# Forgetting-branch gate projection moved between the units of the stick-breaking attention

## The reference

```python
def mixer(h, ...):
    proj = h @ w_in
    (q_r,k_r,v_r,g_r, q_s,k_s,v_s,g_s, q_f,k_f,v_f,g_f, f_logit) = split(proj)
    o_r = retention(rotary(q_r), rotary(k_r), v_r, state)      # 6 heads of 64
    o_s = stick_breaking(q_s, k_s, v_s)                        # 5 heads of 64
    logf = log_sigmoid(f_logit + b_f)
    o_f = forgetting_attention(rms(q_f), rms(k_f), v_f, cumsum(logf))
    o = concat([o_r*silu(g_r), o_s*silu(g_s), o_f*silu(g_f)])
    return o @ w_out
# stick breaking:  A[t,s] = sigmoid(z_ts) * prod_{s<j<t} (1 - sigmoid(z_tj)), s < t
```

## Time and profile before

| | us |
|---|---|
| median of three runs | 3687.98 |
| profiled execution, its time | 3678.38 |
| its span, first to last instruction | 3676.8 |
| TensorE busy | 3204.2 (87%) |
| VectorE busy | 1365.4 (37%) |
| ScalarE busy | 950.5 (26%) |
| GpSimd busy | 597.8 (16%) |

### The profile page before, as it was taken

The page is one execution under the profiler, slowest core; times in us unless marked ns, Lnnn a source line. Parts: engine busy times, 40 slices in busy tenths (PEclk is TensorE's granted clock), DMA queues, the critical chain, the costliest instruction groups (busy, mean ns, idle before and its releaser), DMA issues. The chain is left out here.

```text
span 3676.8 us, 67694 instructions
## 1 busy us (share of the span) xinstructions
PE 3204.2 (87%) x25256; PEld 1989.8 (54%) x25256; DVE 1365.4 (37%) x3002; ACT 950.5 (26%) x1746; POOL 597.8 (16%) x1090
## 2 busy tenths in 40 slices
PE   6999987888998688799989998978889987887998
PEld 4556654555666455444455666545556654554443
DVE  3235086443224444312142350954433244442211
ACT  2012144332224333211020122433322242331110
POOL 0000000444010044400000000004440101452000
PEclk9999988999999799899989999989999997998999
DMA  5011103887120388710120011048861205995102
GB/s 175 18 36 33 50 10 105 265 287 244 38 83 1 117 278 290 249 66 16 46 96 28 28 45 44 1 129 288 284 217 33 72 1 173 295 299 186 57 29 72
DMA packets 268657, 439.67 MB, mean 120 GB/s; under 512 B 48818, under 2 KB 216403, under 8 KB 268339
## 3 DMA queue, kind: packets, MB, share of 16 engines
q1 hardware_dynamic: 205810, 239.96, 20.4%
q0 software_dynamic: 55744, 189.25, 15.6%
q10 hardware_dynamic: 6912, 7.87, 0.6%
HBM read 410.28 MB, written 26.65 MB: 119 GB/s over the span
## 5 line engine op out<-in xcount | busy, mean ns | idle before, releaser
L806 PE MATMUL ps<-W,xT 128*128 128x320 f32 (+7 forms) x5120 | 1482.9, 465 | 11.5 <-DVEq L449 11.5
L806 PEld LDWEIGHTS ps<-W,xT 128*128 128x128 f32 (+1 forms) x5120 | 856.7, 184 | 585.6 <-issue 291.5
L688 POOL DMA_DIRECT2D branch<-in_cache_sb_v_dram x480 | 258.8, 539 | 637.5 <-issue 597.3
L688 POOL DMA_DIRECT2D branch<-in_cache_fox_v_dram x480 | 258.9, 539 | 621.2 <-issue 579.6
L1468 ACT ACTIVATE branch<-ps 128x512 f32<-128x512 f32 x288 | 165.6, 595 | 386.6 <-PE ps L1051 378.2
L1051 PE MATMUL ps<-C,W 128*128 128x128 f32 x1280 | 199.4, 301 | 73.1 <-DMA W<-in_cache_fox_k_dram 26.6
L1051 PE MATMUL ps<-C,branch 128*128 128x128 f32 x1280 | 194.9, 295 | 65.7 <-DMA branch<-in_cache_sb_k_dram 18.0
L1136 PE MATMUL ps<-branch 128*8 128x64 f32 x9920 | 182.2, 234 | 55.9 <-DMA branch<-in_cache_fox_v_dram 27.6
L1073 PE MATMUL ps<-branch,work 128*32 128x512 f32 x896 | 229.9, 631 | 0.8 <-issue 0.2
L1051 PEld LDWEIGHTS ps<-C,W 128*128 128x128 f32 x1280 | 151.0, 151 | 141.0 <-issue 67.4
L1051 PEld LDWEIGHTS ps<-C,branch 128*128 128x128 f32 x1280 | 147.8, 149 | 146.3 <-issue 96.1
(11 more groups left out here) (246 smaller groups left out, 3389.1 us busy)
## 6 DMA issues: line engine op xcount, KB each, us to landing
branch<-in_cache_sb_v_dram POOLq DMA_DIRECT2D x480, 160.0 KB, 4.3
branch<-in_cache_fox_v_dram POOLq DMA_DIRECT2D x480, 160.0 KB, 4.1
W<-in_cache_sb_k_dram SPq DMA_DIRECT2D x248, 160.0 KB, 3.4
W<-in_cache_fox_k_dram SPq DMA_DIRECT2D x248, 160.0 KB
branch<-in_cache_sb_k_dram SPq DMA_DIRECT2D x240, 160.0 KB, 4.2
branch<-in_cache_fox_k_dram SPq DMA_DIRECT2D x240, 160.0 KB, 4.3
W<-in_w_in_dram SPq DMA_DIRECT2D x14, 1280.0 KB, 6.3
W<-in_w_in_dram SPq DMA_DIRECT2D x9, 1536.0 KB, 7.1
```

The source lines that it names most:

```text
L688: pool.dma_start(ringV[:, g % 2, p * DA:(p + 1) * DA], cache[L, bass.ds(pg, 1)].rearrange("a s h d -> s (a h d)"))\
L806: ins = pe.matmul(out, src[:, k, t * P:t * P + R], W[i % 2][:, k, a:z], start=(k == 0), stop=(k == kc - 1), **place)
```

## The change

The nine `fg` tiles are projected within ATT_S, in pieces, in bank 7. Outputs of both attentions are now weighed in bank 6 alone and transposed into bank 7. The pieces and their places (i, h), each behind `turn` of that unit:

- tile 0: two k-steps each at (0,0), (0,1), (0,2), (0,3)
- tile k = 1 to 7: three at (k-1,4), three at (k,0), two at (k,1)
- tile 8 (sample rows): all eight at (7,4)

```diff
+ATT_FILL = {}                      # (i, h) -> (tile, first k-step, end)
+    _at = [(0, 0), (0, 1), (0, 2), (0, 3)] if _k == 0 else [(_k - 1, 4), (_k, 0), (_k, 1)]
+    _cut = [0, 2, 4, 6, KC] if _k == 0 else [0, 3, 6, KC] if _k < SAMPLE else [0, KC]
# banks
-    return 3 + 4 * (n % 2) if seg in IN_RET else n % 3
+    return 3 + 4 * (n % 2) if seg in IN_RET else 7 if seg == "fg" else n % 3
# weights: fq, fv -> W[0], fk -> W[1]; fq loaded once fg is projected
+W_OF = {seg: (0 if seg in ("fq", "fv") else 1 if seg == "fk" else i % 2) ...}
                 load_k(L, kind, 0, 0)
+                if kind == "sb":
+                    load_weights(L, "fq")
                 sp.wait_ge(phase_sem, 4 * ((ATT_S if kind == "sb" else ATT_F) + 1))
# TensorE, attention: weigh
-                    if c == 0 and i >= 2:
-                        pe.wait_ge(att_done[kind], i - 1)
+                    if c == 0 and i >= 1:
+                        pe.wait_ge(att_copied[kind], i)
# TensorE, back: bank 7, and
+                    if i >= 1:
+                        pe.wait_ge(att_done[kind], i)
+                    if kind == "sb":
+                        pe.wait_ge(emptied_dve, evac_count("fg", i + 1))
# TensorE, unit loop
-                    if h == 2 and i >= 1:
+                    if h == 3 and i >= 1:
                         back(t + 1)
                     turn(u)
+                    if kind == "sb" and (i, h) in ATT_FILL:
+                        k, first, end = ATT_FILL[i, h]
+                        if first == 0:
+                            if i >= 1:
+                                pe.wait_ge(att_done[kind], i)
+                            segment_start("fg", k, L)     # waits for tile k-1 emptied
+                        segment_steps("fg", k, first, end)
# ScalarE, unit loop, behind to_sbuf(u)
-                    if h == 1 and i >= 1:
+                    if h == 0 and i >= 1:
                         copy_out(t + 1)
+                    if kind == "sb" and h == 2 and i >= 1:
+                        gate_tile("fg", i)
+                    if kind == "sb" and (i, h) == (0, 4):
+                        gate_tile("fg", 0)
# VectorE, unit loop, behind stick(u)
+                    if kind == "sb" and h == 2 and i >= 1:
+                        gate_tile("fg", i)
+                    if kind == "sb" and (i, h) == (0, 4):
+                        gate_tile("fg", 0)
                     if h == 3 and i >= 1:
                         finish(t + 1)
# both, behind the units
+                if kind == "sb":
+                    gate_tile("fg", SAMPLE)
```

More of the change, by code:

```diff
@@ L62 @@
 TURNED = {"rq": TILES, "rk": TILES, "sq": NT, "sk": NT, "fq": NT, "fk": NT}
+W_OF = {seg: (0 if seg in ("fq", "fv") else 1 if seg == "fk" else i % 2) for i, seg in enumerate(ALL_SEGS)}
 GATE_AT = {"rg": 0, "sg": DR, "fg": DR + DA}
@@ L299, in step_program @@
         squares = cut(work, 2200, HA, HD)
-        logit = cut(work, 2600, TILES, HA)
+        logit = sb("logit", [P, TILES, HA])[:]
         ltmp = cut(work, 2650, TILES, HA)
@@ L578, in _ @@
                 sp.wait_ge(phase_sem, 4 * (DEC_S + 1))
-                load_weights(L, "fq")
+                load_weights(L, "fk")
                 load_decoded(L, "sb")
-                for seg in ALL_SEGS[10:13]:
+                for seg in ALL_SEGS[11:13]:
                     load_weights(L, seg)
@@ L781, in segment_tile, with segment_start @@
             def segment_tile(seg, t, L):
+                segment_start(seg, t, L)
+                segment_steps(seg, t, 0, PLE // P if seg[:2] == "pe" else KC)
+            def segment_start(seg, t, L):
                 i = ALL_SEGS.index(seg)
                 n = i * TILES + t
-                R, N = rows(t), SEG_W.get(seg, 512)
                 if t == 0 and seg == "rq":
@@ L795, in segment_tile @@
                     pe.wait_ge(norm_out, (TILES if seg == "pg0" else 0) + t + 1)
-                back = 2 if seg in IN_RET else 3
+                back = 2 if seg in IN_RET else 1 if seg == "fg" else 3
                 if n >= back:
@@ L800, in segment_tile, with segment_steps @@
                     pe.wait_ge(emptied_dve if s3 in DVE_EVACUATES else emptied_act, evac_count(s3, t3))
+            def segment_steps(seg, t, first, end):
+                R = rows(t)
                 src = pT if seg[:2] == "pe" else xT
                 kc = PLE // P if seg[:2] == "pe" else KC
-                for k in range(kc):
+                for k in range(first, end):
                     for out, a, z in pieces(seg, t):
                         place = dict(tile_position=(0, ROWS if a else 0), skip_group_check=True) if t == SAMPLE else {}
-                        ins = pe.matmul(out, src[:, k, t * P:t * P + R], W[i % 2][:, k, a:z],
+                        ins = pe.matmul(out, src[:, k, t * P:t * P + R], W[W_OF[seg]][:, k, a:z],
                                         start=(k == 0), stop=(k == kc - 1), **place)
-                ins.then_inc(proj_ready, 1)
+                if end == kc:
+                    ins.then_inc(proj_ready, 1)
             def turn_tile(seg, t):
@@ L1210, in _ @@
                 phase_over(pe, PROJ_S)
-                attention(ATT_S)
+                attention(ATT_S, L)
                 decode(DEC_S, L)
@@ L1214, in _ @@
                 phase_over(pe, PROJ_F)
-                attention(ATT_F)
+                attention(ATT_F, L)
                 decode(DEC_F, L)
@@ L1698, in project @@
                             link(dve.tensor_tensor(out, out, gated[0:R, t % 2, :], ALU.add))
[L1699 to L1704, removed]
+                        if seg == "fq" and t == 2:
+                            dve.wait_ge(logf_act, 2)
+                            dve.scalar_tensor_tensor(logf, logit, 0.0, ltmp, ALU.min, ALU.subtract)\
+                                .then_inc(logf_ready, 1)
+                    if seg == "fq":
                         dve.wait_ge(cum_ready, 1)
@@ L1847, in attention @@
                     link(dve.memset(prod[:, SEQ:SEQ + 1], 1.0))
+                    link(dve.memset(logit, 0.0))
                 def stick(u):
```

54 lines of the change are left out of this document (32 added, 22 removed).

## The result

The changed kernel takes 3754.94 us (median of four runs, 3740.71 to 3773.4) where the kernel before, run beside it, takes 3681.19 (3662.14 to 3694.21): a ratio of 1.0199, 95% interval 1.0168 to 1.023. It is slower, as forecast, but by about 74 us where 22 were forecast; 3755 lies above the range of 3670 to 3736.

The account below looks back on a forecast made before the run. The prediction took ATT_S as a chain over VectorE with TensorE close behind. Its terms, 43.4 + 3 + 8.8 + 1.5 - 45.6, made +11 us a layer, +22 in all: 3705 us, range 3670 to 3736.

Parts of the forecast that it names:

- The gate wait: In ATT_S, VectorE's gate of `fg` waits some 2.3 us for ScalarE's sigmoid, seven times.
- the layout: ATT_S instruction times laid out on paper, period by period: 115.6 us from `turn` (1,2) to (7,2), stage +43.4 us.
- Clock in ATT_S: Half clock behind TensorE's gaps in front of `turn` in ATT_S: +3 us a layer (0 to +6).
- the +59 that I gave as a bound: ATT_S growth if no filler found a gap and seven gate waits of 3.1 us came on top.
- the front: ATT_S up to `turn` (1,2): half clock, tile 0's gate and a wait for the emptied bank, +7.3 us.
- the end: End of ATT_S: sample tile, two sigmoid pieces and two products before the last `back`, +3.4 us.
- ATT_F: ATT_F: `back` at head 3 delays VectorE's finish and a chain behind it, +8.8 us (0, or +12 with clock losses).
- 45.6 in the sum: PROJ_F: us removed a layer, from the nine tiles, the `logf` wait, the sums and `fq`'s first tiles.
- the 7.9 for `logf` and the clock behind it: PROJ_F: 4.0 us wait for `logf`, 1.5 on the sums and 2.4 on `fq`'s first tiles removed.
- DEC_S: DEC_S: `fq`'s load holds SyncE's page loads, +2 us (0 to +4.7), less 0.5 for full clock: +1.5.
- Rival 3: Clock and DMA at their upper ends, ATT_S at 46: +23 us a layer, 3725 to 3735 us; chance 0.16.
- rival 1: Engines' slack takes the filler: ATT_S +25 us, -10 a layer, 3664 to 3680 us in all; chance 0.13.

Follow-up runs that it names:

- e1: Changed kernel with the `fg` gate, `back` and `finish` one unit later in ATT_S, all filler kept: 3704.22 us, ratio 1.0059 to the kernel before.
- e3: Changed kernel with 63 dummy transposes in all behind `back` in ATT_S, in TensorE's gaps: 3719.47 us, ratio 1.0118 to the kernel before.
- e10: Changed kernel, filler behind heads 2 to 4, gates behind head 0's `stick`, sigmoid and `back` reordered, ATT_F's `back` at head 2, `out0` load late: 3630.63 us.
- e2: Changed kernel with `back` at head 2 again in ATT_F alone: 3717.69 us, ratio 1.0103 to the kernel before.
- e6: Kernel before with only the `logf` chain moved beside `fq`'s tiles and the sums behind them, `fg` staying in PROJ_F: 3665.97 us, ratio 0.996.
- e5: Changed kernel with the load of `out0` held until PROJ_F's end: 3748.41 us, ratio 1.0173 to the kernel before.
- e9: e8 with each filler piece making only its first k-step, 46 of 72 k-steps a layer left out: 3638.2 us, ratio 0.9902 to the kernel before.
- e4: Changed kernel with each filler piece making only its first k-step, 46 of 72 left out a layer, waits kept: 3719.08 us, ratio 1.0108.
- e8: Changed kernel with the edits of e1, e2 and e5 together: 3668.48 us, ratio 0.9966 to the kernel before.

## Why the prediction was right and wrong

**The direction and its reason were right.** ATT_S is a chain over VectorE with TensorE close behind; the gate waits for a sigmoid that ScalarE's order puts late; and each engine waits in the other's heavy part. The gate wait has the size given (14.0 us in seven, 2.0 each, where I said about 2.3), the first `turn` stands at 7.16 against 7.1, and TensorE's gaps in front of it are 3.35, 2.88 and 2.42 us where the layout has 3.4, 3.0 and 2.5. e1's edit, which takes these waits away, gave back more than any other single one.

**The step that failed is "Clock in ATT_S", +3 (0 to +6).** The mechanism was the right one and its size was not. The layout's +43.4 leaves 20.5 us of ATT_S's +63.9 in layer 1 and 15.3 of +58.7 in layer 2; layer 1 even lies above the +59 that I gave as a bound. The distances from `turn` (k,2) to `turn` (k+1,2) in layer 1, read from the timelines, say where it was lost:

| us, for k = | 1 | 2 | 3 | 4 | 5 | 6 | sum |
|---|---|---|---|---|---|---|---|
| before | 19.6 | 17.1 | 14.8 | 12.4 | 10.0 | 9.3 | 83.2 |
| layout | 25.85 | 23.05 | 20.45 | 18.05 | 15.45 | 12.7 | 115.6 |
| after | 29.3 | 26.0 | 24.3 | 20.1 | 18.0 | 15.3 | 133.0 |
| e3, gaps filled | 26.1 | 23.6 | 21.0 | 18.4 | 18.2 | 15.4 | 122.6 |
| e10 | 22.3 | 19.9 | 17.5 | 15.2 | 13.1 | 11.2 | 99.2 |

In e3 the clock is at its full level through the first four periods, and there each distance comes within about 0.5 us of the layout. So the written order was laid out rightly and takes 87.4 us in these four. The kernel after takes 99.7, and filling the gaps gives back 10.7 of the 12.3 between them. In the last two periods both kernels have half level again and both are 5 us above the layout; that these 5 us are the clock's too is likely and was not tested. The term of +3 stands for 10.4 us shown in layer 1 and 7.2 in layer 2, and perhaps 16 in layer 1. Of the other pieces of the +43.4, the front has +8.9 / +3.4 for +7.3 and the end +5.3 / +5.1 for +3.4.

Half clock grew by 40.0 / 23.9 us. I charged the clock for the first 3 us behind the gap, as wide as the window in the earlier trace rows happened to be, and for little more than the first tiles. The traces show stretches of 6.8 to 10.2 us at the half level around each such gap, and they came for shorter gaps too: the same instruction in the later periods of the kernel after,

```profile
552.06 1.54 PE L986 MATMUL ps<-C,branch 128*128 128x128 f32 x6 [2.88 <-DVE branch L1912]
577.40 1.33 PE L986 MATMUL ps<-C,branch 128*128 128x128 f32 x5 [2.42 <-DVE branch L1912]
601.00 1.11 PE L986 MATMUL ps<-C,branch 128*128 128x128 f32 x4 [1.94 <-DVE branch L1912]
620.45 0.90 PE L986 MATMUL ps<-C,branch 128*128 128x128 f32 x3 [1.48 <-DVE branch L1912]
```

has half level from 551.4 to 558.2, 575.3 to 585.6, 599.2 to 606.0 and 619.7 to 626.5. The window 575 to 585 reads:

```profile
575.00:585.00 10.00, 7.60 (x34) 5.22 (x35) 8.36 (x11) 1.94 (x3) 0.00 (x0) 0.52 0.01 2
```

Ten us at half clock put TensorE some us behind in a period with no slack to catch up. The rule weighed in the prediction (the Trainium skill, "TensorE: Matmul & The Clock Gate", Why this matters for your kernels) names a longer gap than any of these four; by it none would have cost a clock. The measured rows decide, as I had chosen, and even so I charged too little.

**ATT_F: mechanism right, size too small.** TensorE's waits for the exponential and the copy behind it grew as said, by about one us each; the kernel after has 2.4 where the earlier trace rows have 1.37:

```profile
PE ps L1001 <- ACT work L1465: 14.9, 11, 2.4
PE ps L1001 <- ACT branch L1465: 8.8, 5, 2.4
```

Before, the two groups had 11.9 and 6.1 us, so the waits grew by 5.7. The rest of +17.1 / +12.8 goes with the clock: half level 67.3 / 46.9 us instead of 33.1 / 30.7; no run separates the two here. I had "+12 if clock losses follow" as the upper end, and it was too low. e2 takes nearly all of it away with one line.

**PROJ_F: TensorE's part right, an edit not costed.** Without the wait at its end the stage shrank by 44.9 us in both layers, for 45.6 in the sum, and L878 (the cumulative sums) has no wait. The sum came out though e6 gives back only 5.9 / 4.5 us of the 7.9 for `logf` and the clock behind it: in the whole change, 44.9 less the 37.6 of the tiles leaves 7.3. But I gave the order of the weight loads a sentence for `fk` and none for `out0`, whose 2048 KB moved from the middle of the stage to its last us, in front of a store that the barrier waits for: that wait grew by 3.9 / 3.7 us, and e5 gives back 3.4 / 3.1. The rule I cited for DEC_S (the Trainium skill, "DMA: Bandwidth & Descriptors", Issuing engines are not separate DMA queues) is what bears on this place: a load issued by SyncE held a store issued by GpSimd, 6.3 us to landing for 2.3. In DEC_S, where I had used it, +0.3 / +3.1 can't be told from that stage's scatter (312.0 to 326.9 over all these kernels).

**The rest** held: bank 6 alone cost nothing that shows, `fk` came in time. DEC_F's +7.7 in layer 2 has no cause here; that stage scatters from 318.6 to 329.8 over the kernels of this case.

**The sum.** Per layer, the terms were off by +17.5 / +12.3 (ATT_S), -1.2 / +1.6 (DEC_S), +4.6 / +4.4 (PROJ_F), +8.3 / +4.0 (ATT_F) and +0.9 / +7.7 (DEC_F), 60 us in both layers. Rival 3, clock and DMA at their upper ends, was the right one in kind; its ends were the forecast's own bounds, and those were what was wrong. A slip that changed no choice: rival 1's 3668 us is on the footing of the median, 3688 - 20; on the profile's it is 3658.

**Open.** e10's ATT_S is 160 us where TensorE's 116.8 of work before and 37.6 of filler would be 154. How much of what is left, and of e9's length, is coupling of the two engines and how much the clock was not told apart. Nor was it tested what the gate, `back` and `finish` cost each by itself.

## What to carry to other kernels

Filler between the units of a pipeline with two in flight is not judged by idle time in the stage but by what each moved instruction waits for at its place in its engine's order: a gate behind a late sigmoid, with what hung on it, cost 24 us a layer, and the same filler in an order without such waits costs 22.4 to 22.8 us for its 37.6. The layout on paper was good to half a us a period where the clock stayed full; what it lacked was the clock. Where such a layout leaves TensorE a gap that is not there now, price the clock for the whole stretch that a trace shows behind such gaps, in each period, not for the length of the window that was looked at. And list every load that a new buffer assignment moves, up to the ones beyond the stage, and ask which small store or barrier it now lands beside.

## What the runs showed of the hardware

Less work made TensorE's clock lower. With two thirds of the filler left out, half clock in ATT_S rose from 75.3 to 90.3 us in one order of instructions (e4) and from 40.7 to 54.9 in another (e8, e9), so the filler that is taken away gave back only 13 to 21 of its 24.5 us. Dummy transposes in the gaps (e3) kept the clock at 1.00 where it was 0.50 and made the stage shorter by 10.4 / 7.2 us.

Gaps of TensorE of 1.48 to 3.35 us, one in each of the first five periods of the changed ATT_S, each went with 6.8 to 10.2 us at the half level; in e10, where no gap over 0.9 us stands between 479 and 612 us, the clock stays full through that stretch.

An 80 KB store that lands in 2.3 us took 6.3 when a 2048 KB load was issued on another engine's queue just ahead of it, and 2.9 with that load moved away (e5).
